# Channel-major q and k, rotary halves in tiles of their own, and a new order of residual loads in a one-layer decoder step on eight cores

## The chip, the cores and the metric

The kernel runs on the 8 cores of one Trainium2 chip. Each core has a matrix engine (TensorE, in the profile PE, with its weight loads PEld), a vector engine (VectorE, DVE), an activation engine (ScalarE, ACT), GpSimd (POOL) and a queue engine (SyncE, SP) that only issues transfers. Every engine works through its own list of instructions in order; semaphores tie the lists together. Matmuls read on-chip memory (SBUF) and add into PSUM, which has 8 banks of 2 KB in each of 128 partitions. Each core works on its own data and writes its own outputs; nothing passes between cores. The metric is the time of one execution on the device in microseconds, taken on the slowest core.

## What is computed

One layer of a decoder with two head groups side by side. Cut to what matters:

```python
h = rms_norm(x, norm_mix_g)
z = h @ w_in                     # columns: q 1024 | k 256 | v 256 | u_val 1024 | u_gate 1024
q = rope(rms_norm(q, q_norm_g), pos)      # per head of 64: norm over 64, then rotation of
k = rope(rms_norm(k, k_norm_g), pos)      # the halves: x1*cos - x2*sin, x2*cos + x1*sin
a = attn(q, k, v, sinks)         # 16 heads, 4 kv heads, each 128-query block sees its own and
                                 # the previous 128 keys; a learned sink in the denominator
u = u_val * sigmoid(u_gate)      # GLU
c = causal_dwconv(u, conv_w, conv_b)      # 1024 channels, width 31
c = silu(layer_norm(c, conv_ln_g, conv_ln_b))
x = x + concatenate([a, c]) @ w_out
x = x + square(relu(rms_norm(x, norm_mlp_g) @ w_up)) @ w_down    # hidden 8192
```

The prompt has 4 sequences of 2048 rows; in addition 32 single rows ("sample") are each processed against a cache of 128 keys and values and 30 conv rows. Besides x, the new keys, values and conv rows are outputs.

## The kernel before

Each core takes half a sequence: 1024 prompt rows, 128 rows before them (the halo) and 4 sample rows, together 1160 columns of x transposed (`HW`), cut into ten tiles `TT` of up to 128 columns (h, m0 to m7, s).

**Order.** The program is written as a list of instructions through the helpers `dma` (L568), `act` (L581), `tt` (L585), `ts` (L598), `cp` (L603 on ACT, L605 on DVE), `red` (L609), `mm` (L621) and `tr` (L625); in the trace nearly every instruction has one of these lines. `P.add` finds the dependences from the memory ranges that each instruction reads and writes. `schedule` then sets the order on every engine: a list scheduler that takes, of the instructions that are ready by its modelled costs, the one written first. Matmuls between two `P.group()` calls stay together. So neither the written order nor the chip's own timing decides alone what stands behind what, and once set, the order on an engine is fixed.

**Load stage.** The 16 row blocks of x transposed come over SP's queue into four buffers, each is scaled to bf16 (`HT`) and its squares are added into `SS1`. The weights wkv come over POOL's queue. K and V for eight tiles are added up meanwhile, token-major: 128 rows of tokens by 512 columns.

**Q, K, V stage.** The column sums of `SS1` and three fp32 "spreads" of them over all partitions give the row norms (`RTK`, `RB`). Q is computed token-major, for nine tiles 16 x 2 matmuls of 512 columns. For each tile `qk_chain` squares on ACT, forms the rotation on DVE (operations of 1024 columns), sums the squares per head and scales; `fin_q` transposes the tile by eight matmuls into `QT`, with channels on partitions and a pair of heads of 64 rows in each of eight channel blocks. K goes the same way into `KT`. Then come 16 wq loads (POOL; the first two wait for x block 13, the others for the last x block), four loads of the GLU weights wu, and the group of semaphore `cks`: the cached keys (`ckt`, into `KTS`) and the cached values (`cv`, 127 rows, into `CVB`). `sample_a`, which handles the 4 sample rows, begins with a DVE copy of the 4 new keys into `KTS` (4 x 2 columns).

**GLU stage.** For eight channel blocks c, six `u_job`s of 16 matmuls (three pieces of 352, 352 and 356 columns for the gate, then three for the value). Between them stand the attention units (n, gp), 16 of them, one every third job: `unit_a` makes the scores of a query block against the own and the previous key block, four matmuls on 64 rows each into PSUM banks 0 to 3, then an exponential on ACT and a mask multiplication on DVE for each bank; `unit_b` makes values and denominators, eight matmuls of 64 columns, in banks 4 and 5. Conv of block c - 2 runs during block c: `u_done` copies the GLU output four times, shifted, by 16 transfers on SP into `U4[c % 2]` (issued at L918), and each of two `conv_job`s adds 32 matmuls of 32 columns' width.

**Tail and MLP.** `wo_half(dc, 0)` is the attention part of the output projection for row block dc, 24 matmuls of 344 columns, which DVE adds to the residual x block in `XT` (16 `xt` loads on SP). `ln_stats` and `ln_chunk` are the LayerNorm over conv channels, `wo_half(dc, 1)` the conv part with `norm2`; then the MLP, 16 groups of up and down projection.

## Time and profile before

| | |
|---|---|
| time, three runs | 1404.16, 1410.88, 1468.95 us; median 1410.88 |
| profiled execution | 1400.96 us; span of its slowest core (core 2) 1399.4 us |
| spans of the cores | 1388.3 to 1399.4 us |
| busy on core 2: PE, DVE, ACT, POOL | 94%, 53%, 20%, 8% of the span |
| chain that ended last, by engine | PE 83%, transfers 10%, DVE 3%, others 1% or less each |
| granted clock of TensorE, mean | 0.976 to 0.982 of full speed |

The page gives busy time over the whole span. The queries used below cut it: a list of cores; windows, which give the busy time of each engine in a stretch with the granted clock, the busy share of the DMA engines and GB/s; timelines, one engine in order of time, where instructions of one kind that follow one another make a row and the bracket says how long the engine was idle before and what ended it; and groups of instructions by form.

### The profile page before, as it was taken

The page shows a single profiled execution, that of the slowest core. Times are in us where ns is not written, and L with a number is a line of the kernel's source. Part 1 is how long each engine was busy: PE and PEld are TensorE (multiplying, and loading weights), DVE is VectorE, ACT ScalarE, POOL GpSimd, SP SyncE. Part 2 cuts the span into 40 slices and gives each one's busy share as a digit, 9 for nine tenths or more (in the row PEclk, how much of TensorE's full clock was granted, in tenths as well). Part 3 has the DMA queues.
Part 4 walks back from the last instruction along what each step waited for, and adds up shares of the span by engine and source line. Part 5 has one row for each costly group of instructions (what it writes and reads, how often), then busy time and mean ns, then how long its engine had stood idle before and what let it go on. Part 6 is the DMA issues. An engine that isn't in the chain of part 4 may idle for free.

```text
span 1399.4 us, 22368 instructions; the slowest of 8 cores (1388.3 to 1399.4 us)
## 1 busy us (share of the span) xinstructions
PE 1317.3 (94%) x9016; PEld 826.4 (59%) x9016; DVE 742.7 (53%) x851; ACT 279.9 (20%) x429; POOL 112.1 (8%) x200
## 2 busy tenths in 40 slices
PE   5896799999789999999999999999999999999996
PEld 1343355554456666666666666666666666666664
DVE  4874855665375524363453544634536446355365
ACT  3531445644034520001001000010000100100000
POOL 2320000000001100100001001010010000100000
PEclk9988899999999999999999999999999999999998
DMA  9990055749739583526426245163362551633009
GB/s 243 207 136 6 1 90 110 159 88 176 178 46 141 93 165 68 94 36 113 76 46 108 53 82 91 31 121 71 51 106 40 97 91 31 121 59 63 16 7 235
DMA packets 57336, 130.96 MB, mean 94 GB/s; under 512 B 19064, under 2 KB 22012, under 8 KB 57212
## 3 DMA queue, kind: packets, MB, share of 16 engines
q0 software_dynamic: 38880, 90.74, 39.5%
q1 hardware_dynamic: 18356, 38.80, 10.4%
q8 instruction: 73, 1.20, 0.4%
q14 instruction: 27, 0.22, 0.1%
HBM read 202.73 MB, written 10.35 MB: 152 GB/s over the span
## 4 chain that ended last, share of the span: by engine, by line
PE 83%; DMA 10%; DVE 3%; issue 1%; SPq 1%; ACT 1%; POOL 1%; DVEq 0%; ACTq 0%; POOLq 0%
PE psum L621 82%; DMA arena<-xt 3%; DVE arena L585 3%; DMA arena<-cv 3%; DMA arena<-wup 2%; DMA arena<-wq 1%; DMA arena<-arena 1%; SPq L918 1%; ACT arena L581 1%; POOL arena L568 1%; PE psum L625 0%; DVE arena L598 0%; SPq L568 0%; DVEq L379 0%; DVE arena L605 0%
## 5 line engine op out<-in xcount | busy, mean ns | idle before, releaser
L621 PE MATMUL psum<-arena 128*128 128x344 bf16 (+5 forms) x8924 | 1311.6, 322 | 56.0 <-DMA arena<-wkv 17.3
L621 PEld LDWEIGHTS psum<-arena 128*128 128x128 bf16 (+2 forms) x8924 | 820.5, 99 | 542.1 <-issue 121.5
L585 DVE TENSOR_TENSOR arena<-psum,arena 128x1032 f32<-128x1032 f32 (+8 forms) x408 | 426.4, 1050 | 214.5 <-PE psum L621 197.1
L585 DVE TENSOR_TENSOR arena<-arena 128x1032 bf16<-128x1032 bf16 (+10 forms) x364 | 287.2, 807 | 394.4 <-ACT arena L581 381.0
L581 ACT ACTIVATE arena<-psum 128x512 bf16<-128x512 f32 (+7 forms) x150 | 115.7, 786 | 813.1 <-PE psum L621 812.1
L581 ACT ACTIVATE arena<-arena 128x352 f32<-128x352 f32 (+10 forms) x237 | 146.6, 645 | 134.6 <-DVE arena L585 87.2
L568 POOL DMA_DIRECT2D arena<-wup x64 | 33.9, 529 | 409.6 <-PE psum L621 409.6
L568 POOL DMA_DIRECT2D arena<-wdn x64 | 33.9, 531 | 375.6 <-PE psum L621 374.5
L598 DVE TENSOR_SCALAR arena<-arena 128x1160 bf16<-128x1160 f32 (+2 forms) x25 | 15.7, 626 | 16.1 <-DMA arena<-xt 15.0
L603 ACT COPY arena<-psum 128x1024 bf16<-128x1024 bf16 (+5 forms) x18 | 13.2, 771 | 54.7 <-PE psum L625 52.4
L568 POOL DMA_DIRECT2D arena<-wo x16 | 11.3, 704 | 147.6 <-PE psum L621 147.6
L625 PE MATMUL psum<-arena 128*128 128x128 bf16 (+1 forms) x92 | 7.5, 228 | 14.9 <-DVE arena L585 14.9
L568 POOL DMA_DIRECT2D arena<-wu x16 | 8.5, 532 | 149.1 <-PE psum L621 146.0
L581 ACT ACTIVATE arena<-psum,arena 128x512 f32<-128x512 f32 x16 | 11.1, 691 | 38.8 <-PE psum L621 38.8
L609 DVE TENSOR_REDUCE arena<-arena 128x4 f32<-128x256 bf16 (+4 forms) x27 | 17.2, 637 | 0.7 <-ACT arena L581 0.2
L625 PEld LDWEIGHTS psum<-arena 128*128 128x128 bf16 (+1 forms) x92 | 6.1, 105 | 19.2 <-issue 18.0
L568 POOL DMA_DIRECT2D arena<-wkv x16 | 9.6, 603 | 37.6 <-DMA arena<-xt 36.8
L605 DVE COPY arena<-arena 128x4 f32<-128x4 f32 (+2 forms) x12 | 3.6, 301 | 17.0 <-DMA arena<-cv 16.4
L568 POOL DMA_DIRECT2D arena<-wq x16 | 9.0, 617 | 3.8 <-DMA arena<-xt 3.8
L613 POOL MEMSET arena<- 128x32 bf16 (+1 forms) x2 | 0.3, 138 | 67.2 <-PE psum L621 67.2
L581 ACT ACT_TABLE_LOAD x3 | 3.8, 1283 | 8.8 <-DMA arena<-xt 7.4
L605 DVE COPY arena<-psum 128x512 f32<-128x512 f32 (+1 forms) x8 | 4.7, 617 | 0.0
(10 smaller groups left out, 11.9 us busy)
## 6 DMA issues: line engine op xcount, KB each, us to landing
arena<-wdn POOLq DMA_DIRECT2D x64, 512.0 KB, 11.6
arena<-wup POOLq DMA_DIRECT2D x64, 512.0 KB, 6.9
arena<-xt SPq DMA_DIRECT2D x16, 580.0 KB, 10.2
arena<-arena SPq DMA_DIRECT2D x128, 65.8 KB, 5.2
arena<-xt SPq DMA_DIRECT2D x16, 516.0 KB, 16.4
yt<-arena SPq DMA_DIRECT2D x16, 514.0 KB, 9.2
arena<-wu POOLq DMA_DIRECT2D x16, 512.0 KB, 7.7
arena<-wo POOLq DMA_DIRECT2D x16, 512.0 KB, 8.7
```

The costliest lines, as they stand in the source:

```text
L568: return P.add(eng, lambda e: e.dma_start(out=out.ap, in_=in_.ap), reads=[in_], writes=[out], key=key, group=group, final=final, after=aft ...
L581: return P.add("act", lambda e: e.activation(out=out.ap, in_=in_.ap, func=func, bias=b, scale=s), reads=rd, writes=[out], cost=cost("act", ...
L585: return P.add(eng, lambda e: e.tensor_tensor(out=out.ap, in0=in0.ap, in1=in1.ap, op=op), reads=[in0, in1], writes=[out], cost=cost(eng, o ...
L598: return P.add(eng, lambda e: e.tensor_scalar(out=out.ap, in0=in0.ap, scalar1=a, scalar2=b, op0=op0, **kw), reads=rd, writes=[out], cost=c ...
L603: return P.add("act", lambda e: e.copy(out=out.ap, in_=in_.ap), reads=[in_], writes=[out], cost=cost("act", out, [in_]))
L605: return P.add(eng, lambda e: e.tensor_copy(out=out.ap, in_=in_.ap), reads=[in_], writes=[out], cost=cost(eng, out, [in_]))
L609: return P.add("dve", lambda e: e.tensor_reduce(out=out.ap, in_=in_.ap, axis=AX.X, op=ALU.add), reads=[in_], writes=[out], cost=(size(in_) ...
L613: return P.add(eng, lambda e: e.memset(out.ap, val), writes=[out], cost=cost(eng, out, []))
L621: return P.add("pe", lambda e: e.matmul(out.ap, lhsT.ap, rhs.ap, start=start, stop=stop), reads=[lhsT, rhs], writes=[out], cost=c)
L625: return P.add("pe", lambda e: e.transpose(out.ap, in_.ap, ident.ap), reads=[in_, ident], writes=[out], cost=60)
L918: P.add("sp", (lambda src=src, dst=dst: (lambda e: e.dma_start(out=dst.ap, in_=src.ap)))(), reads=[src], writes=[u4()] if i == 0 else [], ...
```

## The change

K for the first 1024 columns and V for six tiles are added up during the loads, the rest of both after them. Q and K are computed channel-major: the weights are the stationary operand and the tokens run along the columns, so no transposes follow. Their channels are sorted so that first halves of the heads (32 channels each, four heads in a tile) lie in one tile of 128 partitions and second halves in another. The rotation then works on whole tiles, with tables of cosines and sines per column (two of 128 x 1160 instead of one of 128 x 1280). Each head's sum of squares comes from a matmul with a block-diagonal matrix `BD`. Since a head is now split over two tiles, a score is the sum of two matmuls on 32 rows. Scores of four kv heads go to four banks in one unit (`unit_s`, one for each query block and key block), values follow per pair (`unit_v`). Scores and values have fixed steps in every block c. Residual loads 4 to 15 wait for the last transfer of `u4` for block 7; three projection halves stand between the convs of blocks 6 and 7, and three more before `ln_stats`.

```diff
+    def rope(ps2, n, c0, g, out, out_f32=None):
...
+        for h in range(2):
+            act(xg(h, nn), ps2(h, nn), AF.Identity, scale=g[h])
+        act(sq((0, 2), nn), ps2((0, 2), nn), AF.Square)
+        ss = ps_f32(6 + i, 1, (n,))
+        P.group()
+        mm(ss(), O128(), EB((c0, c0 + n)), True, False)
+        mm(ss(), BD(), sq(0, nn), False, False)
+        mm(ss(), BD(), sq(1, nn), False, True)
+        act(rs(nn), ss(), AF.Ln, scale=1.0 / 64)
+        act(rs(nn), rs(nn), AF.Exp, scale=-0.5)
+        tt("dve", RA((0, 2), nn), xg((0, 2), nn), bc(COS((c0, c0 + n)), 1, (128, 2, n)), ALU.mult)
+        tt("dve", RBB((0, 2), nn), xg((0, 2), nn), bc(SIN((c0, c0 + n)), 1, (128, 2, n)), ALU.mult)
+        tt("dve", RA(0, nn), RA(0, nn), RBB(1, nn), ALU.subtract)
+        tt("dve", RA(1, nn), RA(1, nn), RBB(0, nn), ALU.add)
...
+            tt("dve", out, RA((0, 2), nn), rb, ALU.mult)
...
-    for i, ti in enumerate(range(4, 10)):
-        P.group()
-        for kc in range(16):
-            q_mm(ti, i % 3, kc)
...
-        fin_q(*pend.pop(0))
-        pend.append(q_chain(ti, i % 3))
+    for p in range(4):
+        for pi, (a, b) in enumerate(PM):
+            acc = ps_f32(2 * (nq % 3), 2, (2, 512))
...
+            for kc in range(16):
...
+                for h in range(2):
+                    mm(acc(h, (0, PW)), WQ(p, kc, (128 * h, 128 * h + 128)), HT(kc, (MC0 + a, MC0 + b)),
+                       kc == 0, kc == 15)
...
+            rope(acc, PW, MC0 + a, GQ, Ref(q.ap[:, p::4, :], QT(p, (a, b)).rngs + QT(4 + p, (a, b)).rngs))
...
+    def unit_s(n, kb):
+        kc0 = MC0 + 128 * (n - 1 + kb)
         P.group()
...
+        for h in range(2):
+            for g in range(4):
+                pr = (32 * g, 32 * g + 32)
+                mm(ps_f32(g, 1, (4, 128))(), KT(h, (kc0, kc0 + 128), p=pr),
+                   QT((4 * h, 4 * h + 4), (128 * n, 128 * n + 128), p=pr), h == 0, h == 1)
...
+            if step < 2:
+                unit_s(c, step)
+            elif step in (3, 4):
+                unit_v(c, step - 3)
...
-        if c == 3:
+        u4_last = u_done(c)
+        if c == 4:
             gate_xt = [P.streams["pe"][-1]]
...
-    for dc in list(range(7)) + list(range(9, 16)):
+    for dc in range(4):
         xt_load(dc)
...
+    gate_xt = [u4_last]
+    for dc in range(4, 16):
+        xt_load(dc)
+    for dc in range(3):
+        wo_half(dc, 0, AT)
     conv_job(7, 0)
     conv_job(7, 1)
...
+    for dc in range(3, 6):
+        wo_half(dc, 0, AT)
     ln_stats()
```

Also changed: tables and parameters come later among the x blocks (after x blocks 6, 10 and 11 instead of 2 and 5); the exponentials of the scores have 12 buffers instead of 8; the new keys leave as one transposed output; the first 11 loads of the down-projection's weights wait for the first `wo_half(dc, 1)`. In the changed kernel the helpers stand 4 lines higher (`mm` is L617, `tt` L581), and `u_done` issues at L875.

On DVE, the stretch around the copy of the new keys into `KTS` (`COPY 128x8`), between the chains of two Q tiles, before:

```order
L585 TENSOR_TENSOR arena<-arena 128x1024
L585 TENSOR_TENSOR arena<-psum,arena 128x1024
L585 TENSOR_TENSOR arena<-arena 128x1024
L585 TENSOR_TENSOR arena<-psum,arena 128x16x32 x2
L609 TENSOR_REDUCE arena<-arena 128x16
L585 TENSOR_TENSOR arena<-arena 128x1024
L605 COPY arena<-arena 128x8
L585 TENSOR_TENSOR arena<-psum,arena 128x1024
```

and now, where a Q job has three operations on both halves and two on one, with the copy behind the subtraction and addition of Q job 4 (the fifth of twelve):

```order
L581 TENSOR_TENSOR arena<-arena 128x2x344 x3
L581 TENSOR_TENSOR arena<-arena 128x344 x2
L581 TENSOR_TENSOR arena<-arena 128x2x344 x3
L581 TENSOR_TENSOR arena<-arena 128x344 x2
L601 COPY arena<-arena 128x8
L581 TENSOR_TENSOR arena<-arena 128x2x344 x3
L581 TENSOR_TENSOR arena<-arena 128x344 x2
```

The copy has stayed among the Q work and still waits for the `cks` loads; behind it stand the last product of Q job 4 and the two products of job 5.

On PE, the end of the GLU stage and the tail before (32x512 is conv, 64x512 the value unit, 128x352 and 128x356 GLU jobs, 128x344 the projection):

```order
L621 MATMUL psum<-arena 64x512 x8
L621 MATMUL psum<-arena 32x512 x32
L621 MATMUL psum<-arena 128x356 x16
L621 MATMUL psum<-arena 32x512 x32
L621 MATMUL psum<-arena 64x512 x8
L621 MATMUL psum<-arena 32x512 x32
L621 MATMUL psum<-arena 128x344 x96
L621 MATMUL psum<-arena 32x512 x64
L621 MATMUL psum<-arena 128x344 x6825
```

and now:

```order
L617 MATMUL psum<-arena 128x352 x16
L617 MATMUL psum<-arena 32x512 x32
L617 MATMUL psum<-arena 64x512 x8
L617 MATMUL psum<-arena 128x356 x16
L617 MATMUL psum<-arena 32x512 x32
L617 MATMUL psum<-arena 128x344 x24
L617 MATMUL psum<-arena 32x512 x32
L617 MATMUL psum<-arena 128x344 x96
L617 MATMUL psum<-arena 32x512 x64
```

Behind the last GLU job (128x356) stand a conv job of block 6, one projection half, the other conv job of block 6, four halves, and then the two conv jobs of block 7; the last value unit has moved ahead of the last GLU job.

On SP, from the sample rows' values to the last residual load, before (L918 is `u_done`, 16 for each block):

```order
L568 DMA arena<-arena 1x16x16 x4
L918 DMA arena<-arena 32x1052 x48
L568 DMA arena<-xt 128x1032 x4
L918 DMA arena<-arena 32x1052 x64
L568 DMA arena<-xt 128x1032 x6
L918 DMA arena<-arena 32x1052 x16
L568 DMA uf<-arena 128x272
L568 DMA arena<-xt 128x1032 x6
```

and now:

```order
L564 DMA arena<-arena 1x16x16 x4
L875 DMA arena<-arena 32x1052 x80
L564 DMA arena<-xt 128x1032 x4
L875 DMA arena<-arena 32x1052 x48
L564 DMA uf<-arena 128x272
L564 DMA arena<-xt 128x1032 x12
```

The six residual loads that stood right ahead of the copies of block 7 are gone from there; twelve stand behind them.

## Rows read from the trace of the kernel before

**Rows 1.** Cores: span and mean granted TensorE clock.

```profile
core 1: 1396.3 us, clock 0.978
core 2: 1399.4 us, clock 0.980
```

**Rows 2.** Windows, core 2: length, busy per engine (instructions), PEclk, DMA share, GB/s.

```profile
57.04:173.45 116.41, 93.36 (x476) 43.49 (x476) 80.27 (x132) 42.99 (x104) 11.61 (x15) 0.87 0.45 61
173.45:333.35 159.90, 159.20 (x1350) 88.26 (x1348) 102.25 (x214) 90.84 (x177) 9.09 (x16) 1.00 0.60 112
333.35:424.00 90.65, 74.39 (x534) 45.09 (x533) 49.58 (x52) 20.52 (x22) 5.62 (x8) 0.91 0.64 134
```

**Rows 3.** Timeline of PE, core 2: start, us, what, [idle before <-releaser].

```profile
121.86 1.01 PE L625 MATMUL psum<-arena 128*128 128x128 bf16 x8 [11.13 <-DVE arena L585]
123.17 8.44 PE L621 MATMUL psum<-arena 128*128 128x512 bf16 x32 [0.30 <-DVE arena L585]
...
336.42 0.83 PE L621 MATMUL psum<-arena 128*32 128x512 bf16 x12 [2.92 <-DMA arena<-arena]
...
364.63 1.90 PE L621 MATMUL psum<-arena 128*32 128x512 bf16 x16 [7.78 <-DMA arena<-arena]
...
396.70 3.60 PE L621 MATMUL psum<-arena 128*128 128x344 bf16 x12 [5.55 <-DVE arena L585]
```

**Rows 4.** Windows of PE: Q tile, value unit, score unit, conv, GLU, projection, sums, spreads.

```profile
131.88:138.79 6.91, 6.91 (x36) 1.00 0.00 0
198.74:199.72 0.98, 0.98 (x9) 1.00 0.98 167
199.72:200.26 0.54, 0.54 (x6) 1.00 1.03 159
209.18:211.02 1.84, 1.84 (x34) 1.00 1.00 250
211.03:213.54 2.51, 2.51 (x20) 1.00 1.04 201
342.67:346.17 3.50, 3.50 (x28) 1.00 1.05 208
60.58:62.68 2.10, 2.10 (x19) 1.00 1.07 169
66.27:68.05 1.78, 1.78 (x7) 1.00 1.00 152
```

**Rows 5.** Timeline of DVE, core 2, at the copy of the new keys.

```profile
119.25 0.19 DVE L605 COPY arena<-arena 128x8 bf16<-128x8 bf16 x1 [16.35 <-DMA arena<-cv]
```

**Rows 6.** Tile cv, core 2.

```profile
DMA to landing us min/median/max: 37.3/37.3/37.3
```

**Rows 7.** Timeline of DVE, core 1, the same copy.

```profile
121.59 0.19 DVE L605 COPY arena<-arena 128x8 bf16<-128x8 bf16 x1 [20.52 <-DMA arena<-cv]
```

**Rows 8.** Groups by form, 57 to 424 us: busy, mean ns of one | idle before.

```profile
L585 DVE TENSOR_TENSOR arena<-arena 128x1024 f32<-128x1024 f32 x8 | 9.7, 1214 | 0.0
L585 DVE TENSOR_TENSOR arena<-arena 128x352 f32<-128x352 f32 x16 | 8.3, 521 | 1.8 <-ACT arena L581 1.8
L581 ACT ACTIVATE arena<-psum 128x512 bf16<-128x512 f32 x64 | 36.0, 592 | 12.8 <-PE psum L621 11.8 <-DVE arena L585 0.9
L581 ACT ACTIVATE arena<-arena 128x352 f32<-128x352 f32 x48 | 23.8, 495 | 28.5 <-DVE arena L585 20.2 <-DVE arena L605 6.9
```

**Rows 9.** Windows, core 2, load stage (columns as in rows 2).

```profile
40.00:50.00 10.00, 6.53 (x29) 2.55 (x30) 9.23 (x10) 5.17 (x5) 3.73 (x6) 1.00 1.02 257
```

**Rows 10.** Timeline of POOL, core 2: the main wq loads.

```profile
53.54 7.41 POOL L568 DMA_DIRECT2D arena<-wq  x14 [3.82 <-DMA arena<-xt]
```

**Rows 11.** Timeline of SP, core 2: residual loads ahead of block 7's copies.

```profile
326.92 8.04 SPq L568 DMA_DIRECT2D arena<-xt  x6
335.81 11.47 SPq L918 DMA_DIRECT2D arena<-arena  x16
```

**Rows 12.** Page, part 6: the copies of the GLU output, us to landing.

```profile
arena<-arena SPq DMA_DIRECT2D x128, 65.8 KB, 5.2
```

**Rows 13.** Windows, core 1, tail up to the second half (columns as in rows 2).

```profile
337.05:419.20 82.15, 72.47 (x534) 44.67 (x533) 49.56 (x52) 20.46 (x22) 5.62 (x8) 0.92 0.65 141
```

More of the change, by code:

```diff
@@ L822, in q_chain @@
[L822 to L835 removed]
+            tt("dve", out_f32, RA((0, 2), nn), rb, ALU.mult)
+            cp("act", out, out_f32)
+        else:
+            tt("dve", out, RA((0, 2), nn), rb, ALU.mult)
@@ L1202, in build_program @@
     late = [P.streams["pe"][-1]]
-    dma("sp", R(nks[:, 0:127, :]), R(ck[:, 1:128, :]), "d2d", group=True, final=True, after=late)
+    dma("sp", R(nks), R(ck[:, 1:128, :]), "d2d", group=True, final=True, after=late)
     dma("sp", R(nvs[:, 0:127, :]), R(cv[:, 1:128, :]), "d2d", group=True, final=True, after=late)
```

463 lines of the change are left out of this document (180 added, 283 removed).

## The prediction

> **What bounds the kernel now.** I read the cores first: core 2 is the slowest of the profiled execution, core 1 comes 3.1 us before it [rows 1]. Then I cut core 2 at the borders of its stages [rows 2]: from the end of the K/V loop to the GLU stage (57 to 173), the GLU stage with conv and attention (to 333), and the tail up to the second half of the output projection (to 424). The reader is to see the PE column beside the length: the GLU stage is full (159.2 of 159.9 us), the stages around it are not. The first holds 93.4 us of matmul in 116.4 at a granted clock of 0.87, the last 74.4 in 90.7 at 0.91. What follows 424 (the projection's second half, the MLP) is not touched, so I look for the change in these three stretches alone.
>
> The timeline of PE names the holes [rows 3]. In the first stretch PE stands 11.13 us at 121.86, named as a wait for DVE; the 32 matmuls behind it take 8.44 us, against 6.91 for 32 alike at full clock [rows 4]. DVE is not slow there: it is held 16.35 us by a copy of 8 columns whose releaser is the load of cv [rows 5]. This copy puts the new K row into KTS for sample_a; it needs the cache K load, which shares its semaphore group with cv. cv takes 37.3 us from issue to landing [rows 6]. On core 1 the same copy ends its wait 2.34 us later [rows 7]. In the tail PE waits 2.92 us and 7.78 us for u4 (conv 6 and conv 7) and 5.55 us for DVE, whose LayerNorm chunks stand ahead of the evacuation of the projection's first half [rows 3].
>
> **The first stretch.** Token-major Q with its transposes goes, and with it DVE's work of about 1.21 us per 1024-column operation [rows 8]. Channel-major Q is 12 jobs of 32 matmuls by 344 columns. A job of 24 such matmuls takes 3.50 us [rows 4], so one takes 4.67. A head norm adds three 344-column matmuls, 0.44. Matmul columns are the same as before (16 x 2 x 1032 x 4 against 9 tiles x 16 x 2 x 512, 0.9 of it), so PE saves little by itself; what counts is where it waits.
>
> The load stage is longer by 2 x 593,920 bytes of tables minus 655,360, less 129,024 of parameters: 0.40 MB, at 257 GB/s [rows 9] 1.6 us. wq waits for the last x (53.54 in before, [rows 10]), the first u weights and cv follow wq, so cv lands 1.6 us later: L = 119.25 + 1.6 = 120.8.
>
> The copy now stands on DVE behind the add of Q job 4's rope. PE's work up to hn7 (the norm of Q job 7) is: column sums 2.10 and spreads 1.78 [rows 4], V's last four tiles (half of 512 columns each) 64 x 0.108 = 6.9, the K remainder (132 columns) 32 x 0.056 = 1.8, three K norms 1.5, nine Q jobs 42.0, seven norms 3.1: 59.2. PE began the sums 7.0 us after the last x landed in before (60.58 against 53.54), so by 62.2 in after; 59.2 more gives 121.4, and a few us of waits on evictions about 125. Then hn7 needs the square of Q7, which ACT can issue only when XG is free, and that needs DVE to pass the copy. From L: copy 0.2, the three two-half operations behind it on DVE (688 columns, 0.87 each between the rows for 352 and 1024 [rows 8]) 2.6, on ACT four of about 0.5 and the square at 0.59 x 688/512 = 0.8: hn7 at L + 5.6 = 126.4. So PE still waits here, whatever it did before, as long as it arrives by 126.
>
> From there: hn7 0.44, Q9 4.67 and the loss behind a wait as above (+1.5, the 8.44 against 6.91), hn8 to hn11 with Q10 and Q11 11.1: 17.7, so L + 23.3 = 144.1 for the start of the GLU work. Per Q job DVE needs 3 x 0.87 + 2 x 0.51 = 3.6 and ACT about 2.8, PE 5.1, so PE sets this run. In before the GLU stage runs without a wait from 173.45, with 5.1 us of its work done by then (one job 2.51, three score units 0.54, one value unit 0.98 [rows 4]): 168.3. Gain **24.2 us**. If cv came in time the GLU stage could start at 62.2 + 59.2 + 16.2 = 137.6, 6.5 earlier; if the evictions, which before does not show in this shape, cost PE 1 us a job more than I allow, it starts some 12 later. These are the two ends.
>
> **The GLU stage.** Same GLU jobs, same conv. Sixteen score units become 8 matmuls of 32 rows by 512 columns instead of 4 of 64. Before has no 32-row matmul; nearest are its own unit, 4 matmuls in 0.54 (two side by side), and conv, 32 matmuls of 32 columns in 1.84, or 0.058 each against 0.216 for a whole one, four side by side [rows 4]. I take 2 x 0.216 + 0.11 = 0.54: nothing. One after another it would be 1.84 a unit, +1.3 x 16 = +20.6. One value unit comes in from the tail, +0.98.
> The Trainium skill ("TensorE: Matmul & The Clock Gate", Part 3, "Measured speedup vs the span model") gives 3.07 times for four row tiles of 32 with 512 columns. That would be an estimate of 0.67 a unit, 2 us in all; no row of before shows it.
>
> **The tail.** xt loads 4 to 15 now follow u4(7) on SP, and three projection halves stand between conv 6 and conv 7. In before six xt loads took SP for 8.04 us right ahead of u4(7) [rows 11], and u4(7), issued over 11.5 us, landed 17.3 after the last issue (347.3 to 364.63), though its median is 5.2 [rows 12]: the six loads of 128 x 1032 x 4 bytes, half a megabyte each, stood in its way. Without them it lands at the end of the last GLU job + 0.7 + 11.5 + 5.2 = +17.4. conv 7 is reached at 1.84 + 3.50 + 1.84 + 4 x 3.50 = +21.2. No wait. After conv 7 (3.7) come 11 halves 38.5, three stats of two fp32 matmuls at 1.78/3, 3.6, and I leave 0.8 for DVE: 67.8 against 90.65, a gain of **22.9**, 21.9 after the value unit. If u4(7) still needs 17.3 after its issue, conv 7 waits 8.3 and loses 1.5 to the clock: +10. xt(4) is needed near +21 to +24 and lands near the first; the others, 2.1 us each at the 257 GB/s above, come faster than one per 3.5. Conv 7's sums (a square, then an add of 1032 columns, about 1.2 each by the row for 1024 [rows 8]) lie under a half of 3.5. The first wdn loads now wait for the first job of the second half; fifteen more jobs, 52 us, stand between them and the MLP: nothing.
>
> **Sum.** Core 2: 1399.4 - 24.2 - 21.9 = 1353.3. Core 1's copy is 2.34 later, and its time behind the start of the second half is 1396.3 - 419.2 = 977.1 against 975.4 on core 2 [rows 1, 13]: 424.0 - 46.1 + 2.3 + 977.1 = 1357.3. The profiled execution took 1400.96, 1.56 over its span, so 1358.9; two of the three runs of before lie 0.2 and 0.7% above the profiled one (the third 4.9%), so I add 3: **1362 us**.
>
> **The rivals.**
> (a) u4(7) or the LayerNorm chain still holds PE in the tail, +10: 1372. For it: other loads, the projection's weights, run at the same time; against it: the median of 5.2. Chance 0.12.
> (b) The 32-row matmuls do not run side by side: +20.6, 1383. For it: no row shows them; against it: 64-row and 32-column ones do. Chance 0.08.
> (c) cv is off the path, since it lands before DVE comes to the copy: up to -6.5, 1356. For it: the spread of the landing over cores (119.25, 121.59) and PE's own 125 lie close together; against it: DVE stood 16 us at the copy. Chance 0.10.
> (d) The other side: the score banks. A unit now writes all four score banks, and each must be read by ACT (0.592) before the next unit, while ACT also has three 0.495 operations per GLU piece [rows 8]: 3.9 us, against 4.4 to 5.0 of matmul between two units (a GLU job with a conv job, or two GLU jobs [rows 4]). If that work comes too late to lie beside them, PE waits the 3.9 and loses 1.5 to the clock, at sixteen units 86 us: 1448. It puts the kernel above before from 3.1 us of loss per unit on, and over 2% above from 4.8. Against it: in before the units use the same four banks every third job, and PE has 0.7 us idle in the whole stage [rows 2]. Chance 0.07.
> The Trainium skill ("TensorEngine Tiling (Array Packing)", "PSUM Bottleneck") says that after a 4x faster packed matmul the PSUM copy may become the limit and that both ACT and DVE should evacuate; here ACT alone reads the scores, and before shows no such wait.
> (e) The change doesn't do what it says: the gain comes back as waits (ACT evictions between Q jobs, u4), 1395 to 1410. For it: the trace has no eviction of this shape, and DVE and ACT had 80 and 43 us of work in the first stretch [rows 2]; against it: the sums per job. Chance 0.05.
>
> **How the numbers follow.** The forecast holds 0.58, with 1350 to 1372 as its own range (both sides of waits of a few us, 0.3% between runs). With (a), (b) and (c) it is 0.88; the range 1347 to 1388 takes them in and leaves (d) and (e) out. About 2% of the median, 1410.88, is what a measurement of this kernel can tell from no change: faster lies below 1383. The forecast, (a), (c) and half of (b) are there: 0.84. Same: half of (b), (e) and a part of (d) with fewer us per unit, 0.12. Slower 0.04.
>
> **What would show it.** In the profile after: the 8-column copy on DVE still ends with cv, near 121, and PE has its one hole of the first stretch ahead of hn7, 1 to 6 us; if PE stops earlier, my order of the queues is wrong. The GLU stage begins at 144 (139 to 147) and lasts 160 to 162; a length of 180 is (b), PE waits for ACT at L617 score matmuls are (d). The tail is 66 to 70 us with no DMA wait over 1 us in it; a wait at conv 7 is (a). Wrong altogether would be a GLU stage that starts after 160.

## The result: 1370 us, faster by 2.5%

The changed kernel takes 1370.17 us (median of four runs, 1369.23 to 1373.32), the kernel before 1407.52 us in the same comparison; the ratio is 0.9747, with a 95% interval of 0.9707 to 0.9787. Forecast were 1362 us and faster by over 2%; the time lies inside the range, 8 us above the forecast. The experiments below ran on other chips, each beside runs of the kernel before, so they are compared by their ratios. Times here and below are medians of all executions of a kernel, while the ratios leave out those in which the cores of one die ran at a lower clock, such as the 1468.95 us among the four of the kernel before.

The cores of the profiled execution (1371.09 us), span and granted clock:

```profile
core 2: 1362.0 us, clock 0.987
core 5: 1369.5 us, clock 0.987
core 6: 1367.8 us, clock 0.983
```

Core 2, the slowest before [rows 1], gained 37.4 us and is now next to the fastest; core 5 sets the time. Its stages by windows (length, busy time of PE, PEld, DVE, ACT, POOL with instructions, granted clock, transfer share, GB/s), as [rows 2] of before, but the first from the end of the loads' matmuls to the first scores, and the last from the second half of the projection to the end:

```profile
61.53:147.55 86.02, 78.19 (x529) 51.69 (x531) 48.51 (x72) 41.25 (x90) 10.44 (x13) 0.93 0.62 78
147.55:315.37 167.82, 166.62 (x1477) 90.47 (x1477) 110.27 (x229) 101.64 (x199) 8.51 (x15) 1.00 0.52 106
315.37:384.00 68.63, 68.33 (x526) 43.09 (x526) 47.71 (x50) 18.94 (x21) 5.61 (x8) 0.98 0.76 172
384.00:1362.00 978.00, 957.65 (x6535) 637.51 (x6533) 473.66 (x417) 103.69 (x102) 71.35 (x133) 0.99 0.48 82
```

The GLU stage ends at 315.4 instead of 333.4, the tail is 68.6 us instead of 90.7 and nearly full, and the stretch that the prediction took as untouched is 2.6 us longer than before (975.4).

The timeline of PE on core 2 has one large hole left:

```profile
129.80 18.36 PE L617 MATMUL psum<-arena 128*128 128x344 bf16 x115 [7.38 <-ACT arena L577]
148.42 2.98 PE L617 MATMUL psum<-arena 128*128 128x352 bf16 x19 [0.26 <-ACT arena L577]
152.10 3.09 PE L617 MATMUL psum<-arena 128*128 128x352 bf16 x24 [0.70 <-ACT arena L577]
155.43 210.16 PE L617 MATMUL psum<-arena 128*128 128x356 bf16 x1828 [0.24 <-DVE arena L581]
```

It stands where the prediction put it, ahead of the norm of Q job 7, and behind it is still the copy that waits for cv (timeline of DVE, core 2; as [rows 5]):

```profile
124.35 0.19 DVE L601 COPY arena<-arena 128x8 bf16<-128x8 bf16 x1 [17.20 <-DMA arena<-cv]
124.52 7.47 DVE L581 TENSOR_TENSOR arena<-arena 128x688 f32<-128x688 f32 x10
```

From 155 to 366 us the matmuls run without a wait that counts. The loads from x to cv are later than before: the last x block (the wait of wq, as [rows 10]) lands 3.3 us later, at 56.87, and cv needs 37.6 us (page of the transfers, core 2, KB each and us to landing):

```profile
56.87 7.40 POOL L564 DMA_DIRECT2D arena<-wq  x14 [6.18 <-DMA arena<-xt]
```

```profile
arena<-ckt POOLq DMA_DIRECT2D x1, 254.0 KB, 16.5
arena<-cv POOLq DMA_DIRECT2D x1, 254.0 KB, 37.6
```

The same amount of data, the cached keys, lands in 16.5 us. What makes core 5 slow, and core 6, stands in their timelines of PE: two waits for loads on core 5, and on core 6 one for DVE ahead of the statistics.

```profile
418.34 80.42 PE L617 MATMUL psum<-arena 128*128 128x344 bf16 x534 [3.48 <-DMA arena<-wo]
501.39 12.41 PE L617 MATMUL psum<-arena 128*128 128x344 bf16 x84 [2.63 <-DMA arena<-wup]
```

```profile
350.63 23.10 PE L617 MATMUL psum<-arena 128*128 128x344 f32 x132 [5.00 <-DVE arena L581]
```

None of these waits has a price in the prediction's sum, which takes the second half as core 1 had it before, 57.7 us.

### The profile page after: what moved, and what is told of

Same layout as the page of the kernel before. It is cut to its first block, busy times and chain, and to the rows that moved or that the text cites. A ratio compares the mean times of both kernels' runs of the same rounds, so it can differ in the third digit from the quotient of the medians.

```text
span 1369.5 us, 22766 instructions; the slowest of 8 cores (1360.2 to 1369.5 us)
## 1 busy us (share of the span) xinstructions
PE 1302.9 (95%) x9241; PEld 840.4 (61%) x9241; DVE 715.9 (52%) x803; ACT 288.6 (21%) x434; POOL 112.4 (8%) x199
## 3 DMA queue, kind: packets, MB, share of 16 engines
q1 hardware_dynamic: 18492, 39.20, 10.8%
## 4 chain that ended last, share of the span: by engine, by line
PE 84%; DMA 11%; DVE 2%; issue 1%; POOL 1%; ACT 1%; SPq 0%; DVEq 0%; ACTq 0%; POOLq 0%
PE psum L617 84%; DMA arena<-xt 3%; DMA arena<-cv 3%; DVE arena L581 2%; DMA arena<-wo 2%; DMA arena<-wup 2%; DMA arena<-wq 2%; POOL arena L564 1%; ACT arena L577 1%; DVE arena L594 0%; SPq L564 0%; DVEq L379 0%; ACTq L379 0%; DVE arena L601 0%; POOLq L379 0%
## 5 line engine op out<-in xcount | busy, mean ns | idle before, releaser
L617 PE MATMUL psum<-arena 128*128 128x344 bf16 (+7 forms) x9241 | 1302.9, 316 | 52.3 <-DMA arena<-wkv 24.0
L617 PEld LDWEIGHTS psum<-arena 128*128 128x128 bf16 (+2 forms) x9241 | 840.4, 99 | 514.4 <-issue 100.2
L581 DVE TENSOR_TENSOR arena<-arena 128x1032 bf16<-128x1032 bf16 (+12 forms) x367 | 299.8, 835 | 404.4 <-ACT arena L577 389.1
L581 DVE TENSOR_TENSOR arena<-psum,arena 128x1032 f32<-128x1032 f32 (+7 forms) x381 | 403.3, 1064 | 187.7 <-PE psum L617 182.1
L577 ACT ACTIVATE arena<-psum 128x512 bf16<-128x512 f32 (+7 forms) x173 | 124.7, 741 | 818.1 <-PE psum L617 817.6
L577 ACT ACTIVATE arena<-arena 128x352 f32<-128x352 f32 (+9 forms) x194 | 139.5, 732 | 99.5 <-DVE arena L581 64.7
L577 ACT ACTIVATE arena<-psum,arena 128x344 f32<-128x344 f32 (+6 forms) x58 | 32.2, 575 | 83.6 <-PE psum L617 62.0
L564 POOL DMA_DIRECT2D arena<-cv x1 | 4.6, 4576 | 0.0
## 6 DMA issues: line engine op xcount, KB each, us to landing
arena<-wdn POOLq DMA_DIRECT2D x64, 512.0 KB, 10.7
arena<-arena SPq DMA_DIRECT2D x128, 65.8 KB, 3.6
yt<-arena SPq DMA_DIRECT2D x16, 514.0 KB, 12.3
```

What stands on the lines that cost most here:

```text
L564: return P.add(eng, lambda e: e.dma_start(out=out.ap, in_=in_.ap), reads=[in_], writes=[out], key=key, group=group, final=final, after=aft ...
L577: return P.add("act", lambda e: e.activation(out=out.ap, in_=in_.ap, func=func, bias=b, scale=s), reads=rd, writes=[out], cost=cost("act", ...
L581: return P.add(eng, lambda e: e.tensor_tensor(out=out.ap, in0=in0.ap, in1=in1.ap, op=op), reads=[in0, in1], writes=[out], cost=cost(eng, o ...
L617: return P.add("pe", lambda e: e.matmul(out.ap, lhsT.ap, rhs.ap, start=start, stop=stop), reads=[lhsT, rhs], writes=[out], cost=c)
```

## The experiments

All kernels, from the traces of all eight cores of one execution each (least to most). The tail is counted from 2.5 us behind the start of the last GLU matmul, 2.3 us later than in the windows above, as the expectations count it; the MLP to the start of its last matmul.

| kernel | first GLU job starts | tail | second half | MLP | ratio to before (95%) |
|---|---|---|---|---|---|
| before | 154.1–158.9 | 78.1–88.3 | 56.0–57.7 | 904.4–907.4 | 1 |
| after | 146.3–151.7 | 65.8–72.9 | 56.0–61.2 | 904.1–907.0 | 0.9747 (0.9707–0.9787) |
| e1 after, cv apart | 135.8–138.8 | 65.8–73.6 | 56.0–62.3 | 904.1–905.9 | 0.9698 (0.9668–0.9727) |
| e2 before, cv apart | 137.1–140.4 | 78.3–89.7 | 56.0–57.8 | 904.4–906.3 | 0.9888 (0.9858–0.9919) |
| e3 before, new tail | 152.9–157.2 | 66.6–75.0 | 56.0–59.9 | 904.4–905.7 | 0.9909 (0.9876–0.9941) |
| e4 after, old tail | 145.0–150.2 | 77.0–84.1 | 56.0–60.6 | 904.6–907.5 | 0.9836 (0.9804–0.9869) |
| e5 after, score rows in turn | 143.6–149.9 | 65.8 | 56.0–62.5 | 904.1–904.4 | none |
| e6 e1, xt 4 first | 134.4–139.9 | 65.8–74.9 | 56.0–62.4 | 904.1–907.3 | 0.9689 (0.9646–0.9731) |
| e7 e1, wdn spread | 136.3–139.1 | 65.8–76.2 | 56.0 | 910.9–914.8 | 0.9736 (0.9692–0.9781) |
| c1 e6, e7, tables late | 130.5–133.9 | 65.8–78.1 | 56.0 | 909.1–913.6 | 0.9705 (0.9665–0.9745) |
| e8 e6, wo behind xt 4 | 136.1–138.3 | 65.8–69.6 | 56.0–62.8 | 904.6–905.3 | 0.9696 (0.9672–0.9720) |
| e9 e1, tables late | 130.4–134.2 | 65.8–72.7 | 56.0–63.2 | 904.1–904.9 | 0.9658 (0.9630–0.9686) |
| e10 after, cv 112 rows | 135.0–140.3 | 65.8–69.9 | 56.0–62.4 | 904.2–906.2 | 0.9687 (0.9663–0.9712) |
| c2 all in order | 130.8–134.4 | 65.8–69.7 | 56.0 | 904.6–905.9 | 0.9629 (0.9613–0.9645) |

Of e5 one execution alone can be compared (1362.88 us), so it has no ratio. In before's layout (before, e2, e3) a rest of the Q work lies behind the first GLU job, so that column compares only within a layout; ends of the GLU stage are given in the text where the two are compared.

### What holds the first stretch: cv

In the changed kernel:

```diff
-    dma("pool", CVB(p=(0, 127)), R(cv[:, 1:128, :].rearrange("s k d -> k s d")), "cks", group=True, after=[wqd[15]])
+    dma("pool", CVB(p=(0, 127)), R(cv[:, 1:128, :].rearrange("s k d -> k s d")), "cvl", group=True, after=[wqd[15]])
```

> The changed kernel, in which the load of cv has a semaphore of its own, so that the copy of the new keys waits for the cached keys alone (they land 16.5 us after issue, cv 37.6 us). The order on every engine stays the same. Theory (the cv wait still holds the first stretch): the copy runs when DVE comes to it, near 107 us instead of 122.8 to 127.6; the idle 4.7 to 11 us of PE ahead of the norm of Q job 7 go, with some 1.5 us behind them; the GLU stage starts 7 to 10 us earlier (138 to 141 instead of 146 to 152) and the time falls from about 1370 to about 1362. Rival (PE is held there by ACT's and DVE's evictions of the channel-major Q, and the cv wait only covers it): the idle time moves to other Q jobs and the time changes by less than 2 us.

Measured: 1357.05 us, 0.9698. The timeline of PE on core 2 has no hole from the spreads to the first GLU job:

```profile
60.13 75.65 PE L617 MATMUL psum<-arena 128*128 128x388 f32 x535 [0.46 <-ACT arena L577]
136.05 2.98 PE L617 MATMUL psum<-arena 128*128 128x352 bf16 x19 [0.27 <-ACT arena L577]
```

The GLU stage starts 10 to 13 us earlier. By the ratios 0.5% (7 us) of it arrive at the end, with intervals that still overlap; in the two profiled executions the slowest core ends 10.8 us earlier. More cores now wait in the tail (below), but how much of the gain goes there is not shown. The evictions do not hold PE: the rival falls. The same edit in the kernel before:

> The kernel before with the same edit alone: cv on a semaphore of its own. Theory (the change gains 24 us in the first stretch, partly because less work stands behind the copy, partly because PE has more to do before it): here only the wait itself goes, 11.1 us idle and 1.5 us behind it; the GLU stage starts near 143 instead of 155.7 and the time falls from 1405 by about 12.5 to about 1392. Rival (nearly the whole gain of the first stretch is this wait): the GLU stage starts 20 us or more earlier and the time falls by 20 to 24 us.

Measured: 1384.26 us, 0.9888, thus 15.7 us of 1405. The GLU stage ends about 17 us earlier (by the same count, 317.6 to 321.5 against 334.9 to 339.4 us), between theory and rival: more than the 12.6 of the wait and the slow matmuls behind it. So of the some 18 us by which the changed kernel's GLU stage ends earlier (315.5 to 320.9) the layout is not the whole cause. In the mean of the eight cores the stage ends at 336.4 in before, 319.5 in e2, 318.4 in after and 306.3 in e1 (305.0 to 308.0). So without the wait the new version ends it 13 us earlier than the old one, and the wait costs the old layout 17 us there and the new one 12, although cv lands 5 us later in it. That the new layout loses less because PE has nine Q jobs to do before it runs out of work is argued, not tested. These three numbers give the whole gain of 18 us whatever the causes (13 + 17 - 12), so the sum is no check of them.

Why is cv slow? Half of the question is how it is cut:

```diff
-    dma("pool", CVB(p=(0, 127)), R(cv[:, 1:128, :].rearrange("s k d -> k s d")), "cks", group=True, after=[wqd[15]])
+    for r0, r1, k in ((0, 112, "cks"), (112, 127, "cvr")):
+        dma("pool", CVB(p=(r0, r1)), R(cv[:, 1 + r0:1 + r1, :].rearrange("s k d -> k s d")), k, group=True, after=[wqd[15]])
```

> The changed kernel with the load of cv in two pieces: 112 of the 127 rows of each sample in the same semaphore group as the cached keys, the other 15 behind them on a semaphore of their own. The copy of the new keys on DVE waits for the cached keys and the 112 rows, still 7/8 of cv. In the changed kernel cv (127 partitions) and the cached keys (128 partitions) are both 254 KB, and land 37.6 and 16.5 us after issue. Theory (a transfer over 127 partitions runs through one of the 16 transfer engines; 508 rows of 512 bytes one after another): 112 partitions spread over all 16 and land 16 to 20 us after issue; the copy no longer waits 14.5 to 20.8 us, the hole of 5 to 11 us in PE closes, and the time falls as with cv apart, by 6 to 8 us against the changed kernel (a ratio to before near 0.970). Rival (small rows of 512 bytes that are converted on the way are slow on any engine): the 112 rows need 7/8 of the time, about 33 us, and the time falls by 2 to 4 us.

Measured: 1355.7 us, 0.9687. Transfers of core 2 (KB, us to landing), and the copy on DVE:

```profile
arena<-cv POOLq DMA_DIRECT2D x1, 224.0 KB, 18.1
arena<-cv POOLq DMA_DIRECT2D x1, 30.0 KB, 2.0
```

```profile
105.67 0.19 DVE L601 COPY arena<-arena 128x8 bf16<-128x8 bf16 x1 [1.49 <-DMA arena<-cv]
```

224 KB over 112 partitions land in 18.1 us, 254 KB over 127 in 37.6: it is the number of partitions, not the size of the rows. One line gives the whole gain of e1, with the copy still waiting for cv.

### The tail alone, and the rest without it

The tail's part of the change in the kernel before (residual loads, three and three halves, gates, as in the change's diff), and the changed kernel with the old tail:

> The kernel before with only the tail of the change: residual loads 0 to 3 behind block 4, 4 to 15 behind the last copy of block 7, three projection halves between conv 6 and conv 7 and three more before the LayerNorm statistics, the LayerNorm chunks behind half 6, the first loads of the down weights behind the second half's first job. Q, K, scores as before. Theory: the tail falls from 78 to 88 us (cores of before) to about 67 to 69, and the slowest core by about 20 us: 1385 to 1388. Rival (the loads that are moved give the gain back later, as waits of the second half for wo and of the MLP for wup): the tail is short, but the second half and the MLP get 3 to 8 us longer and the time falls by 12 to 16 us, to 1390 to 1394.

> The changed kernel with the tail of the kernel before: residual loads in the old order and gated by block 3, conv 7 right behind conv 6, LayerNorm chunks behind half 3, no gate on the down weights. Channel-major Q and K and the 32-row scores stay. Theory: the tail is 78 to 88 us again with waits for the copies of the GLU output ahead of conv 6 and conv 7, and the time is about 1388 (18 to 20 more than the changed kernel). Rival (the two parts are not additive, since the earlier end of the first stretch moves the loads out of each other's way): less than 10 us more.

Measured: 0.9909 for the tail alone (13 us of 1405) and 0.9836 for the rest alone (23 us). Their sum, 2.55%, is the 2.53% of both: the two parts add up within the intervals (for what e4 leaves out see below). The tail was worth 13 us and not the 20 of the first of the two expectations, as its rival says, but only partly for its reason. In e3 five cores have the forecast tail of 66.6 us; cores 0, 3 and 7 have 74.6, 75.0 and 71.5. On core 0, with three halves and not four ahead of conv 7, this conv waits for u4:

```profile
356.45 36.92 PE L621 MATMUL psum<-arena 128*32 128x512 bf16 x268 [6.18 <-DMA arena<-arena]
```

And the old tail is near 90 us only on some cores: in before it is 78 to 80 on four, 83 to 88 on the others. The expectation of e4, waits for u4 again and some 20 us, is not met: seven cores have 77 to 78.5, with this one wait (core 2), and only core 6, with 84.1, waits for u4.

```profile
374.79 65.51 PE L617 MATMUL psum<-arena 128*128 128x344 bf16 x431 [10.06 <-DVE arena L581]
```

But e4 has the old tail not to the letter: the scheduler, free to set the order, puts six projection halves ahead of conv 7 where before has four. So against e4 the new order removes the wait for DVE behind the LayerNorm chunks, 11 to 13 us (77 to 78.5 against 65.8) with what it costs in clock: from 374.79 to 379.00 the granted clock is 0.50. In before that wait is 5.55 us, and a wait for u4 stands beside it, 10.7 us in two parts on core 2 [rows 3] and 4.13 us on core 1:

```profile
360.13 27.44 PE L621 MATMUL psum<-arena 128*32 128x512 bf16 x196 [4.13 <-DMA arena<-arena]
```

### The scores

```diff
-        for h in range(2):
-            for g in range(4):
+        for g in range(4):
+            for h in range(2):
                 pr = (32 * g, 32 * g + 32)
```

> The changed kernel with the two loops of a score unit exchanged: the two 32-row matmuls that add into one bank follow one another on the same 32 rows, instead of four neighbours on four different groups of rows. The same 8 matmuls. In the changed kernel a unit takes 0.54 us between GLU jobs (0.85 to 0.87 at the start of the stage). Theory (neighbours on different rows run side by side, two on the same rows one after the other, and the engine issues in order): a unit takes 0.9 to 1.2 us, 16 units 6 to 10 us, and the GLU stage grows from 167.8 us by that. Rival (the order doesn't matter, the engine overlaps what it can): 0.54 us and no change.

Measured: no difference that counts. Windows of PE on core 2, one unit each: of the changed kernel, and of this one

```profile
301.10:301.64 0.54, 0.54 (x12) 1.00 1.05 191
```

```profile
302.72:303.27 0.55, 0.55 (x13) 1.00 0.97 180
```

(The counts take in neighbours whose ends reach into the window.) Eight matmuls of 512 columns would take 8 x 0.216 = 1.73 us one after another; they take 0.54 or 0.55, 3.2 times as fast. From the first score to its end the GLU stage takes 168.0 us against 167.9, not 6 to 10 us more. The rival holds: the order of rows does not matter here. In the traces of both kernels four of a unit's eight matmuls start within 0.02 us, and the other four 0.23 us later, also where the two on the same rows are issued in turn. In this execution the tail is 65.8 us on all eight cores, which the next section explains.

### Waits in the tail: which load is issued first

On five cores of e1 the tail is 70 to 74 us: DVE waits for residual block 4 ahead of half 4's addition, and the sums of conv 7 stand behind it. Two steps, on top of e1:

```diff
     gate_xt = [u4_last]
-    for dc in range(4, 16):
+    gate_xt = [xt_load(4)]
+    for dc in range(5, 16):
         xt_load(dc)
```

> The changed kernel with cv on a semaphore of its own (1357 us) and residual load 4 alone behind the last copy of block 7: loads 5 to 15 wait until it has landed. With cv alone apart five cores have a tail of 70 to 74 us and three one of 65.8; on the slow ones DVE waits for residual block 4 ahead of half 4's addition, and the sums of conv 7 and the statistics stand behind it. Theory (twelve loads at once share the core's transfer rate, so the first lands late): block 4 lands 3 to 5 us after the gate, the wait of 5 to 6 us of PE ahead of the statistics goes on all cores, the tail is 65.8 to 67 everywhere and the time falls by 4 to 7 us, to 1350 to 1353. Rival (what is late is the gate itself, the last copy of block 7): the tail stays at 70 to 74 on several cores and the time at 1355 to 1359.

Measured: 1357.43 us, 0.9689; three cores still have 67.9 to 74.9. The theory falls: alone, too, block 4 lands late on some cores. What parts the cores is seen in their timelines of SP and POOL, on core 0 (slow) and core 6:

```profile
324.12 19.11 SPq L564 DMA_DIRECT2D arena<-xt  x12
```

```profile
323.15 0.71 POOL L564 DMA_DIRECT2D arena<-wo  x1 [6.30 <-PE psum L617]
```

```profile
319.40 11.28 SPq L564 DMA_DIRECT2D arena<-xt  x12
```

```profile
320.09 0.71 POOL L564 DMA_DIRECT2D arena<-wo  x1 [6.30 <-PE psum L617]
```

On core 0 the wo load that half 3 releases is issued 0.97 us ahead of block 4, and DVE waits for that block:

```profile
334.49 1.23 DVE L581 TENSOR_TENSOR arena<-psum,arena 128x1032 f32<-128x1032 f32 x1 [10.69 <-DMA arena<-xt]
```

On core 6 it is issued 0.69 us behind, and DVE waits for PE alone. In the changed kernel core 6 is the one core with the order of the first kind (wo 335.72, block 4 336.46) and the one with a long tail. Over all cores of after, c1, e1, e5, e6, e7, e9 and e10, 64 in all, DVE idled 8.5 to 12.7 us ahead of half 4's addition wherever wo was issued 0.4 us or more ahead of block 4 (17 cores, none of them in e5), 4.2 to 5.7 where it was ahead by less than 0.3 (4 cores), and 2.3 to 4.9 where block 4 came first (43). (These idle times include the wait for PE's sums, so the expectation below, which has 2.4 or less for the last kind, was too narrow.) The next edit, on top of the last, fixes the order:

```diff
-            wo2.append(wo_load(*wo_left.pop(0)))
+            wo2.append(wo_load(*wo_left.pop(0), after=gate_xt if (half, dc) == (0, 3) else ()))
```

> The kernel of the run before last on residual block 4 (cv apart, loads 5 to 15 behind block 4; 1357 us) with one more wait: the load of wo that projection half 3 releases waits until residual block 4 has landed. In five profiled executions of 8 cores each, DVE waited 4 to 13 us for residual block 4 on those cores alone where this wo load was issued ahead of it (0.04 to 1.6 us ahead), and 2.4 us or less where it was issued behind. Theory (the two loads race, and the one issued first takes the transfer engines): with the order fixed no core waits over 2.5 us for block 4, PE's wait of 4 to 6 us ahead of the statistics is gone everywhere, the tail is 65.8 to 67 us on all 8 cores, and the time is 1349 to 1353. Rival (the order of issue is a sign of a late core, not the cause; the load itself is slow where the memory is shared): some cores keep tails of 70 to 75 us, the time stays at 1355 to 1358.

("The run before last" is the kernel just shown.) Measured: DVE idles 2.5 to 4.7 us ahead of half 4's addition on all eight cores, so the wo load under way is what made block 4 late. The tails are 65.8 or 65.9 us on five cores, 67.7 and 68.1 on two, and 69.6 on core 4, where DVE waited two additions later, for block 6 (issued at 329.42, landed at 343.22):

```profile
343.31 1.23 DVE L581 TENSOR_TENSOR arena<-psum,arena 128x1032 f32<-128x1032 f32 x1 [6.71 <-DMA arena<-xt]
```

What block 4 no longer costs, block 6 can cost. The time did not follow: 1357.19, 0.9696. Seven cores lose 1.5 to 6.8 us in the second half, and one of them is the slowest.

### Waits of the second half: six loads in a row

```diff
-        if dc == 0:
-            gate_wdn = [P.streams["pe"][-1]]
+        if dc in (1, 4, 7, 10, 13):
+            gate_wdn.append(P.streams["pe"][-1])
```

and six more gates by jobs of the up projection, each for one load.

> The changed kernel with cv on a semaphore of its own (1357 us) and the first 11 loads of the down weights released one by one: five by jobs 1, 4, 7, 10 and 13 of the projection's second half, six by the first jobs of the up projection, instead of six in a row at the beginning of the second half. Theory (the six loads put the loads of wo behind them: 22.7 to 23.7 us to landing against a median of 8.4): the waits for wo of 2.7 to 3.6 us near 410 us and those for wup near 492 us go, the second half takes 56 us on all cores instead of 56 to 62.3, and the time falls by 4 to 6 us, to 1351 to 1353. Rival (wo is late because the residual loads are still under way or because the cores share the memory): the second half stays at 57 to 62 us, the time within 2 us of 1357.

Measured: the second half is 56.0 us on all eight cores, as the theory has it, and the MLP 911 to 915 instead of 904 to 906, which is more than the second half gained: 0.9736 against 0.9698 of e1, though these two intervals overlap. The six later loads now share the transfer engines with the up weights and the copies of the caches from input to output, and PE waits there (core 5):

```profile
497.37 14.10 PE L617 MATMUL psum<-arena 128*128 128x344 bf16 x84 [8.53 <-DMA arena<-wup]
```

A wait moved, not removed. Which of the two brings the wait, the six loads or the copies, is not separated: c2 below moves both and has an MLP of 904.6 to 905.9 us.

The row itself is not new. POOL on core 1 before, where the row begins 1.6 us into the second half and the wo load behind it lands 21.6 us after issue, and on core 5 after, where it begins 4.4 us into it:

```profile
420.83 2.74 POOL L568 DMA_DIRECT2D arena<-wdn  x5
427.15 0.70 POOL L568 DMA_DIRECT2D arena<-wo  x1 [3.58 <-PE psum L621]
```

```profile
391.10 2.81 POOL L564 DMA_DIRECT2D arena<-wdn  x5 [2.77 <-PE psum L617]
394.63 0.70 POOL L564 DMA_DIRECT2D arena<-wo  x1 [0.72 <-PE psum L617]
395.33 0.63 POOL L564 DMA_DIRECT2D arena<-wdn  x1
```

The change's gate adds the sixth load (in before the first of them goes in the GLU stage) and moves the row 2.8 us nearer to that wo load, which then takes 23.6 us. But e4, which has no gate and the row of five, has second halves of 58.6 to 60.6 us on three cores, too (core 3):

```profile
428.76 80.57 PE L617 MATMUL psum<-arena 128*128 128x344 bf16 x534 [2.73 <-DMA arena<-wo]
```

So e7 shows that the row causes the waits; that the gate made them longer is not shown.

### Tables, and a version from all of it

```diff
-        if kc == 12:
-            dma("sp", COS(), R(tab_d[:, 0:HW]), "cos", after=[xd[10]])
-            dma("sp", SIN(), R(tab_d[:, HW:2 * HW]), "sin", after=[xd[11]])
+    dma("sp", COS(), R(tab_d[:, 0:HW]), "cos", after=[xd[14]])
+    dma("sp", SIN(), R(tab_d[:, HW:2 * HW]), "sin", after=[xd[15]])
```

First together with the edits of e6 and e7 (c1), then on top of e1 alone (e9):

> All of it in one: cv apart, residual load 4 ahead, down weights spread, and the tables of cosines and sines behind the last x blocks instead of between them. Theory: 1357 less 4 to 7 less 4 to 6, and 2 to 3 less for x blocks that land earlier: 1341 to 1349. Rival for the tables (they are then late for the rotation of K, and PE waits for the norms of Q): nothing or a loss of 1 to 3 us in the first stretch against the kernel with cv apart, where the first GLU job begins at 136 to 139 us.

> The changed kernel with cv apart (1357 us) and the two tables of cosines and sines (1.19 MB) behind x blocks 14 and 15 instead of behind 10 and 11; nothing else. In the run with all loads moved the first GLU job began at 130.5 to 133.9 us, with cv alone apart at 135.8 to 138.8. Theory (the tables stand among the last x blocks and hold the load stage up by more than the 0.40 MB that the change adds): the last x block lands 4 to 5 us earlier than the 54.8 to 57.8 us of the changed kernel, the first GLU job begins at 130 to 134, and the time falls by 3 to 6 us, to 1351 to 1354. Rival (the 6 us came from other edits or another execution): first GLU job at 136 to 139, time 1355 to 1359.

Measured: c1 1358.25 us, 0.9705, outside the 1341 to 1349 expected (the MLP of e7 takes back what the start gains); e9 1352.02, 0.9658, as expected, though its interval overlaps that of e1. The first GLU job begins 5 us earlier in both than in e1. The last x block of e9 on core 2 lands at 49.88:

```profile
49.88 7.41 POOL L564 DMA_DIRECT2D arena<-wq  x14 [2.96 <-DMA arena<-xt]
```

7.0 us before the changed kernel's and 3.7 before the old one's. K's rotation still has its tables in time. But cv does not come earlier by as much. POOL on core 2 issues it at 86.68 in the changed kernel and at 85.20 in e9:

```profile
86.68 4.58 POOL L564 DMA_DIRECT2D arena<-cv  x1
```

```profile
85.20 4.58 POOL L564 DMA_DIRECT2D arena<-cv  x1
```

The last version has cv apart, tables late, block 4 first with wo behind it, five down-weight loads along the second half and six at its end, and the three copies of caches behind the sixth MLP group instead of the first:

> A version from all findings: cv apart, tables behind the x blocks, residual block 4 ahead of the others and of the wo load of half 3, the first five loads of the down weights one by one along the second half and the next six together at its end (not along the up projection, which cost 10 us), and the three copies of caches from input to output, 1.5 MB, behind the sixth group of the MLP instead of the first. Theory: first GLU job at 131 to 134, tail 66, second half 56, MLP 904, so that the slowest core is at 1340 to 1346 and the time at 1342 to 1348. Rival (the loads only push each other about, so that the MLP gives it back as a wait for wup as in the run with the down weights spread): MLP 908 to 915, time 1350 to 1358.

Measured: 1348.88 us, 0.9629 (0.9613 to 0.9645), 1.2% under the changed kernel. The stages come out near what was foreseen (the MLP 904.6 to 905.9 instead of 904) but for one tail of 69.7, on core 4 again; the slowest core ends at 1347.2, and both this and the time miss the expected ranges by about 1 us.

## Why the prediction held, and where it was short

**The hole ahead of hn7.** Right in place and in what makes it, larger than the 1 to 6 us given (7.38). From the copy to the norm it took 5.45 us (124.35 to 129.80; worked out 5.6), from there to the first scores 17.75 (17.7). Wrong was L: 124.35 on core 2 and 126.8 on core 5 instead of 120.8. The step that failed is the load stage, 0.40 MB at 257 GB/s or 1.6 us. The last x block came 3.3 us later, and cv 1.8 more behind it. e9 shows why bytes were not the measure for x: the tables cost the last x block 5.7 us where they stood (mean of the eight cores, against e1), and behind the x blocks PE has no wait for them. But it does not show why cv was late. By the same means cv is issued only 1.4 us earlier in e9, so the prediction's step from the last x block to cv, one shift for both, doesn't hold there, and the cause of cv's 5.1 us stays open. That the hole comes from the wait for cv is shown by e1 and e10. The Trainium skill ("DMA: Bandwidth & Descriptors", "Why a DMA increments its semaphore by 16 and not by 1") says that a transfer runs on the largest number of engines, up to 16, that divides the size of the slowest dimension on both sides, here the partitions, so on one for 127; it names an exception on Trainium2, in which some copies issued by GpSimd run 127 partitions on all 16. The 37.6 us for 127 partitions, 18.1 for 112 and 16.5 for 128 agree with the rule and not with the exception, though no view here shows which engines carried them.

**The gain of the first stretch.** 24.2 us forecast; the GLU stage of core 2 ends 18.0 us earlier with 0.98 more in it. L accounts for 3.5 of the rest, three small waits and the like at the start of the GLU stage (167.8 us against 166.0) for 1.8. The 160 to 162 us that the prediction names as a sign leave out the 5.1 us of the stage's work that its own sum counts; with them it is 166.0. The stage begins at 147.55 on core 2, just outside the 139 to 147 given.

**Scores.** Taken at nothing, and nothing it was: 0.54 us. Rivals (b) and (d) fall: on none of the eight cores does PE stand idle ahead of a score unit, and the waits for ACT of 0.26 and 0.70 us at the start of the stage on core 2 are ahead of GLU jobs. That before shows no such wait, as (d) says, was a misreading: ahead of 173.45, where its windows begin, score matmuls wait for ACT (PE on core 2 before).

```profile
161.49 0.86 PE L621 MATMUL psum<-arena 64*128 64x512 bf16 x2 [0.76 <-ACT arena L581]
165.12 0.61 PE L621 MATMUL psum<-arena 64*128 64x512 bf16 x2 [2.77 <-ACT arena L581]
167.52 1.04 PE L621 MATMUL psum<-arena 64*128 64x512 bf16 x4 [1.79 <-ACT arena L581]
```

The estimate of 0.67 us by the 3.07 times of the Trainium skill ("TensorE: Matmul & The Clock Gate", Part 3) was a little high; 0.11 of it is what the prediction added for the unit's own cost, and 0.54 is 3.2 times.

**The tail.** 67.8 us worked out, 68.6 measured on core 2. The load that waits for u4(7) was issued 18.1 us behind the last GLU job (17.4), and conv 7 began at 21.4 (21.2), with no wait. But "xt(4) is needed near +21 to +24 and lands near the first" was the weak place: it was given no price. On core 6 the wo load, issued 0.74 us earlier, put block 4 late, and this cost 7 us. Rival (a) had the price, +10, but named u4; what came was a residual block. The 22 us gained on core 2 are those of a core that was slow in the tail: four cores of before have 78 to 80 us by the table's count, and e3 puts the tail's worth for the slowest core at 13 us.

**What follows 424.** "Not touched" was wrong of the time. On core 5 the second half is 61.2 us instead of 56.0 to 57.7, and PE waits there for wo. The gate on the down weights was costed at nothing: I asked when they are needed, not what they displace. They go six in a row, and e7 shows by spreading them that the row is what makes wo late. The gate is not shown to be the cause of the extra 3.5 us, since five in a row stand in before as well and e4 loses nearly as much without the gate.

**The sum.** The forecast for the slowest core was 1357.3; it was 1369.5. Of the 12.2 us, 6.5 are a later start of the second half (386.7 against 380.2), 3.5 the second half itself, and 2.6 the stretch from the last matmul's start (14.7 us against 12.0 on core 1 before); the MLP is 0.4 shorter. The last matmuls of six cores, core 5 not among them, lie within 4.6 us, and the stores of y take 12.3 us to landing on the slowest core instead of 9.2. That the one causes the other is not shown, and cores 4 and 7 speak against it: their stores land in 6.8 and 6.2 us, and the stretch is 17.9 and 16.0 us long. All these misses but the MLP's have the same sign; the time stays in the range because each is a few us. In core 2's own account, 1353.3 against 1362.0: 3.5 by L, 1.8 by the GLU stage, 0.8 by the tail, 2.6 behind it.

## What to carry to other kernels

When a load's wait is on the path, ask what issued just before it on any queue, and how many partitions it spans, before asking how many bytes there are: here 127 partitions instead of 112 cost cv 20 us, tables in the wrong place cost the last x block 5.7, and a load issued a microsecond too early costs the tail 5 to 7. Look for that row of loads in the kernel before, too, ahead of blaming the change. A gate that moves loads out of one stage must be costed in the stage into which it releases them. An edit whose gain depends on such a race should be priced over all cores; the slowest of eight meets the worst case.

## What the runs showed that I had not expected

What DVE waits ahead of one addition differs by 4 to 10 us (2.3 to 4.9 against 8.5 to 12.7) by whether a 512-KB load was issued behind the 516-KB one that it needs, or 0.4 us or more ahead of it. Two matmuls on the same 32 rows in turn cost no more than on different rows: 0.55 us a unit against 0.54. And the outcome of such a race changes from one execution to the next: without the wait for cv five cores have a late residual block in e1 and one in e10, with it one in after and none in e5. So one execution does not show that removing the wait made block 4 late.
